# The second half of a transformer block dealt out again over five engines: gate rows, up weights, rotation, ada_t pages

## The reference

```python
mod = silu(c) @ ada_w + ada_b
shift1, scale1, gate1, shift2, scale2, gate2 = split(mod)
h = rms_norm(x, norm1_gain) * (1 + scale1) + shift1
r_q, r_k, r_v, r_g, s_q, s_k, s_v = split(h @ w_in)          # 7 x 512 columns
y_ret = head_group_norm(retention(rotary(r_q), rotary(r_k), r_v)) * silu(r_g)
y_sb  = rms_norm(stick_breaking(norm(s_q), norm(s_k), s_v))  # weights from log sigmoids
x = x + gate1 * (concat(y_ret, y_sb) @ w_out)
h2 = rms_norm(x, norm2_gain) * (1 + scale2) + shift2
x = x + gate2 * peer(h2, w_query, sub_keys, expert_down, expert_up)
```

## Time and profile before

| | |
|---|---|
| median of 3 runs | 1330.65 us (1329.43 to 1332.24) |
| profiled execution, its own time | 1334.88 us |
| its span, first to last instruction | 1333.1 us |
| busy share of PE, DVE, ACT, POOL | 96, 74, 55, 23% |
| mean granted clock of PE | 0.976 of full |
| PE's share of the chain that ended last | 91% |
| DMA share in 200 to 240, 240 to 260 us | 0.90, 0.96 |
| waits of PE from 200 to 600 us | none over 0.1 us |

### The profile page before, as it was taken

One profiled execution on the slowest core, in us unless ns is written; L12 is line 12 of the kernel. 1 busy time (PEld: TensorE's weight loads), 2 busy tenths in 40 slices (PEclk: granted clock), 3 DMA queues, 4 the chain that ended last, 5 costly groups with the idle time before them and its releaser, 6 DMA issues.

```text
span 1333.1 us, 19834 instructions
## 1 busy us (share of the span) xinstructions
PE 1273.6 (96%) x7918; PEld 1135.7 (85%) x7918; DVE 991.3 (74%) x1714; ACT 729.2 (55%) x1130; POOL 302.8 (23%) x186
## 2 busy tenths in 40 slices
PE   3797989999999999999999999999989999999998
PEld 3675879999999999999888888888877788899996
DVE  6988878889999889994767777676676465755554
ACT  3664544555555599993554444455455455554443
POOL 0135100088876887540000000000000022000000
PEclk8898999999999999999999999999989997999999
DMA  9964659877777778889887878787654441555551
GB/s 369 358 245 171 217 178 324 308 223 237 237 221 226 225 220 281 271 275 350 332 306 272 303 272 303 274 293 281 225 183 157 161 163 40 189 184 193 184 189 77
DMA packets 138286, 317.10 MB, mean 238 GB/s; under 512 B 24783, under 2 KB 71120, under 8 KB 132306
## 3 DMA queue, kind: packets, MB, share of 16 engines
q1 hardware_dynamic: 101106, 265.42, 55.4%
q0 software_dynamic: 23072, 16.86, 6.7%
q10 hardware_dynamic: 14016, 33.56, 6.6%
HBM read 280.61 MB, written 35.20 MB: 237 GB/s over the span
## 4 chain that ended last, share of the span: by engine, by line
PE 91%; DVE 5%; DMA 1%; ACT 1%; issue 1%; DVEq 0%; SPq 0%; ACTq 0%
PE ps L632 12%; PE ps L633 11%; PE ps L634 11%; PE ps L645 11%; PE ps L644 11%; PE ps L646 11%; PE ps L610 3%; PE ps L611 3%; PE ps L612 3%; PE ps L922 1%; PE ps L974 1%; DVE arena L1729 1%; DMA wring<-in_peer_up 1%; PE ps L993 1%; DVE pages L1729 1%; DVE w_lo L1649 1%
## 5 line engine op out<-in xcount | busy, mean ns | idle before, releaser
L1649 DVE TENSOR_TENSOR w_lo<-wring,w_hi 128x1024 fp32r<-128x1024 f32 (+1 forms) x404 | 492.6, 1225 | 173.6 <-ACT w_hi L1184 169.6
L1184 ACT CAST w_hi<-wring 128x1024 fp32r<-128x1024 f32 (+1 forms) x404 | 418.9, 1044 | 247.2 <-PE ps L634 148.2
L632 PE MATMUL ps<-hT_hi,w_hi 128*128 128x256 f32 x1344 | 377.8, 281 | 0.0
L634 PE MATMUL ps<-hT_hi,w_lo 128*128 128x256 f32 x1344 | 377.5, 281 | 0.0
L633 PE MATMUL ps<-hT_lo,w_hi 128*128 128x256 f32 x1344 | 377.4, 281 | 0.0
L1601 POOL DMA_INDIRECT gates_of_second<-late x128 | 245.8, 1920 | 134.8 <-DMA gates_of_second<-zeros 55.1
L634 PEld LDWEIGHTS ps<-hT_hi,w_lo 128*128 128x128 f32 x1344 | 256.0, 190 | 0.0
L644 PE MATMUL ps<-w_hi,a_hi 128*128 128x512 f32 x640 | 251.8, 393 | 2.7 <-DVE w_lo L1649 2.7
L632 PEld LDWEIGHTS ps<-hT_hi,w_hi 128*128 128x128 f32 x1344 | 253.9, 189 | 0.3
L645 PE MATMUL ps<-w_lo,a_hi 128*128 128x512 f32 x640 | 252.7, 395 | 0.0
L633 PEld LDWEIGHTS ps<-hT_lo,w_hi 128*128 128x128 f32 x1344 | 252.5, 188 | 0.2
(11 more groups left out here) (316 smaller groups left out, 1466.5 us busy)
## 6 DMA issues: line engine op xcount, KB each, us to landing
wring<-in_peer_down SPq DMA_DIRECT2D x32, 2048.0 KB
wring<-in_peer_up SPq DMA_DIRECT2D x32, 2048.0 KB
wring<-in_w_in SPq DMA_DIRECT2D x12, 2048.0 KB
pages<-in_ada_t POOLq DMA_DIRECT2D x32, 512.0 KB, 5.0
acts_by_expert<-pages ACTq DMA_DIRECT2D x32, 512.0 KB
peer_arena<-acts_by_expert SPq DMA_DIRECT2D x32, 512.0 KB, 8.7
wring<-in_w_up SPq DMA_DIRECT2D x8, 2048.0 KB
wring<-in_w_down SPq DMA_DIRECT2D x8, 2048.0 KB
```

The source lines that it names most:

```text
L632: pe.matmul(o, hi[:, k, :], hT_hi[:, k, :], start=(k == 0), stop=False)
L634: mm = pe.matmul(o, lo[:, k, :], hT_hi[:, k, :], start=False, stop=(k == KC - 1))
L1184: act.copy(split_part(kind, w_hi, u, width(kind, j)), part_of(kind, wring[:, n % RING, :], u, width(kind, j))).then_inc(split_hi, 1)
L1649: dve.tensor_tensor(lo, part_of(kind, wring[:, n % RING, :], u, width(kind, j)), hi, ALU.subtract)\
```

## The change

Ten or so pieces of work change places; the arithmetic stays.

- The pages come in another order: gate1 first, then shift2 and scale2 in two halves, then gate2. The second modulation is made in two halves (`late_modulation`), the second one between the halves of `h_round(3)`.
- POOL's second block of the rotation waits for the second group's `sb_logs`.
- PE makes three parts of R_V, not two, before `log_stays(1)`; R_G's first part goes ahead of the rotated turn, its second behind it; `turn_y(0)` goes ahead of `kept_values(1)`; the rows of gate1 go from between the output parts to behind `turn_y(1)`, those of gate2 from the query products to behind down product 18.
- ACT and DVE splits follow. DVE's `h_round(2, half 0)` goes ahead of the sums over the retention values.
- SP issues the first up weights before the wait for `gates_added` and before the second table's first piece.

The diff, cut to the places that the prediction speaks of:

```diff
-LATER_TILES = [*range(3 * KC, 5 * KC), *range(2 * KC, 3 * KC), *range(5 * KC, 6 * KC)]
+LATER_TILES = [*range(2 * KC, 3 * KC), *[which * KC + half * KC // 2 + k for half in range(2) for which in (3, 4) for k in range(KC // 2)],
+               *range(5 * KC, 6 * KC)]
...
                 acts_back(j)
-            sp.wait_ge(gates_added, 16 * PK * PH)
-            second_gates_back(0)
             for u in range(2):
                 sp.wait_ge(gates_stored[u], 16 * (P // 32))
             first_gates_back(0)
             weights(NTH["ex", 0])
+            sp.wait_ge(gates_added, 16 * PK * PH)
+            second_gates_back(0)
+            first_gates_back(1)
             second_gates_back(1)
-            first_gates_back(1)
             weights(NTH["ex", 1])
...
-            by_tokens("win", R_V, parts=[0, 1])
+            by_tokens("win", R_V, parts=[0, 1, 2])
             log_stays(1)
...
             stick_values(0)
-            token_parts("win", R_V, [2, 3])
+            token_parts("win", R_V, [3])
+            by_tokens("win", R_G, parts=[0])
             pe.wait_ge(S["rot_ready"], 2)
...
             turn_round(lambda k, b: h_tok[:, b, k * P:(k + 1) * P], KC)
-            by_tokens("win", R_G, parts=[0])
+            token_parts("win", R_G, [1])
             copied(2)
             head_scores(4, 0).then_inc(S["ret_scores"], 1)
             stick_values(1)
-            token_parts("win", R_G, [1])
             pe.wait_ge(S["ret_decayed"], 1)
             head_scores(4, 1).then_inc(S["ret_scores"], 1)
+            token_parts("win", R_G, [2])
             kept_values(0)
-            token_parts("win", R_G, [2, 3])
-            kept_values(1)
+            token_parts("win", R_G, [3])
+            pe.wait_ge(S["ret_decayed"], 2)
             pe.wait_ge(S["y_ready"], 1)
             turn_y(0)
+            kept_values(1)
             h_stands(2, 0)
-            out_part(0, 0)
-            out_part(0, 1)
-            gate_rows(M_GATE1, 4, 1)
-            out_part(0, 2)
+            for u in range(PARTS):
+                out_part(0, u)
             pe.wait_ge(S["y_ready"], 2)
             turn_y(1)
-            out_part(0, 3)
+            gate_rows(M_GATE1, 4, 1)
             h_stands(2, 1)
...
-                if j == 1:
-                    gate_rows(M_GATE2, 6, 2)
-                if j == 2:
-                    pe.wait_ge(S["gate_out"], 2)
                 key_scores(j - 1)
...
+            pe.wait_ge(S["sub_out"], 4)
+            gate_rows(M_GATE2, 6, 2)
             pe.wait_ge(S["sel_ready"], PH)
...
-            h_round(3, gain=column(modc, M_SCALE2), shift=column(modc, M_SHIFT2))
+            h_round(3, gain=column(modc, M_SCALE2), shift=column(modc, M_SHIFT2), only=0)
+            act.wait_ge(S["mod_ready"], 4)
+            h_round(3, gain=column(modc, M_SCALE2), shift=column(modc, M_SHIFT2), only=1)
...
+                if b == 1:
+                    pool.wait_ge(S["sb_ls"], 2)
                 own(pool.tensor_tensor(dst[:, :, 0, :], src[:, :, 0, :], cos, ALU.mult))
...
+            def late_modulation(half):
+
+                first, count = half * KC // 2, len(FIRST_TILES) + (half + 2) * KC
+                take_columns(M_SHIFT2 + first, M_SHIFT2 + first + KC // 2, count)
+                own(take_columns(M_SCALE2 + first, M_SCALE2 + first + KC // 2, count))
+                modulation(half + 3, M_SCALE2, G_2, first, KC // 2)
...
             dve.wait_ge(S["ret_y_out"], 2)
...
-            h_round(2, only=0)
             dve.tensor_tensor(yr, yr, over_heads(4), ALU.subtract).then_inc(S["y_centered"], 1)
...
             split("wout", 1, parts=[2, 3])
+            sum_pages(3)
+            late_modulation(0)
...
-                if b == 1:
+                if b == 0:
+                    sum_pages(1)
+                else:
                     dve.wait_ge(S["x1_ready"], 2)
...
             split("wq", 0, parts=[1])
+            sum_pages(1)
             h_round(3, gain=column(modc, M_SCALE2), shift=column(modc, M_SHIFT2), only=0)
             split("wq", 0, parts=[2, 3])
+            sum_pages(3)
+            late_modulation(1)
             h_round(3, gain=column(modc, M_SCALE2), shift=column(modc, M_SHIFT2), only=1)
```

More of the change, by code:

```diff
@@ L1290, in _ @@
             weight_exp(0)
-            split("win", R_V, parts=[1])
+            split("win", R_V, parts=[1, 2])
             log_break(1)
-            split("win", R_V, parts=[2, 3])
+            split("win", R_V, parts=[3])
             take_win(S_V)
@@ L1409, in _ @@
                     take_scores(3)
+                if j == TURN_AFTER:
+                    act.wait_ge(S["gate_turned"], 2)
+                    act.copy(GATE2, psf[:, 6 * 512:6 * 512 + D]).then_inc(S["gate_out"], 1)
                 if j >= 1:
@@ L1856, in _ @@
             sb_mask(0)
-            split("win", R_V, parts=[1])
-            sum_pages(2)
+            split("win", R_V, parts=[1, 2])
             sb_logs(1)
-            split("win", R_V, parts=[2, 3])
+            split("win", R_V, parts=[3])
             sum_pages(1)
@@ L1894, in _ @@
             dve.tensor_tensor(ys, ys, head_gain(2), ALU.mult).then_inc(S["y_ready"], 1)
+            split("wout", 0, parts=[0])
+            sum_pages(2)
+            h_round(2, only=0)
             split("wout", 0, parts=[1])
-            sum_pages(1)
             dve.wait_ge(S["ret_y_out"], 2)
```

42 lines of the change are left out of this document (17 added, 25 removed).

## The result

The changed kernel took 1314.9 us, median of four runs (1312.8 to 1318.8), beside 1330.0 for the one before: ratio 0.9888, 95% interval 0.986 to 0.9917. The forecast was 1324.0 in a range of 1318 to 1330. In two later samples of the same kernel the medians were 1323.6 (11 runs, ratio 0.9936, 0.9906 to 0.9966) and 1318.3 (12 runs, 0.9927, 0.9892 to 0.9963). Over all 28 runs the median is 1318.3, against 1329.7 over 93 later runs of the kernel before (one of 1551 left out). The gain is real in each sample. That it is larger than the forecast's 6.6 (a ratio of 0.995) is clear in the first sample alone; the intervals of the two later ones hold 0.995 as well. Most of this text is on where the rest comes from.

What follows compares the result with a forecast made beforehand. TensorE, busy 96% of the span, was taken as the bound, so only its waits and low-clock stretches counted. The terms summed to -6.6, from 1330.65 to 1324.0 us, range 1318 to 1330.

Steps and rivals of the forecast that it cites:

- Terms 1 to 4: Second logarithm's wait gone -8.8; first output product's wait gone -4.3; out_block's new wait +1.0; pages in DVE's slots +0.2.
- Term 5: First query product: PE waits 2.4 for hT_lo behind three pages and half a modulation, then low clock 1.7; +4.1.
- Term 6: Up weights: the second gates' first piece, now issued behind them, delays weighing and ACT's start before the up-projection; +1.2.
- at no cost: Pages, gate rows and GATE2's copy same in number; GATE2's rows move behind down product 18, where PE has no waits.
- the stall hidden (1): DVE runs ahead, so the wait for hT_lo in the first query weight is hidden; 1320.0 us, chance 0.16.
- the head start lost (2): Transfers rather than PE set the pace between 200 and 260, so time won earlier is waited away; 1329, chance 0.13.
- the lock (3): Shared-port lock lengthens the second rotation and margins at output product and out_block are missed; 1328.5, at worst 1332; chance 0.10.
- the late gates (4): First up product waits for gates_of_second's piece, landing more than 20.5 after issue; slower, 1334; chance 0.07.

Runs made afterwards that it cites:

- a_no_pool_wait: The changed kernel without POOL's wait for sb_ls ahead of its second rotation; 1322.9 us in one run.
- b_gate2_late: The kernel before with only GATE2's row products and ACT's copy moved behind down product 18; 1323.4 us (10 runs), ratio 0.9964.
- b_rows_behind: The kernel before with GATE2's row products behind the first key scores instead of ahead of them; 1317.5 us in one run.
- b_gate2_late2: b_gate2_late profiled and timed again; 1328.3 us (12 runs), ratio 0.998.
- a_pages_rows_early: a_pages_out with GATE2's row products, ACT's copy and PE's wait for it back between the query products; 1318.5 us (8 runs), ratio 0.9923.
- a_rows_extra: The changed kernel with a second, unused set of GATE2's 8 row products at their old place between the query products; 1329.1 us (10 runs), ratio 1.0012.
- a_pages_out: The changed kernel with SP's old order at the up weights and two page sums moved from between h_round(3)'s halves to earlier slots; 1312.7 us (four runs).
- a_again: The changed kernel, unaltered, profiled a second time and timed again; median 1323.6 us.

## Why the prediction was wrong

Its walk was right and its total was not. None of the three signs that it named as its own refutation came: out_block started at 165.7 and not later than 168, a stall stood within the first query weight, and from 210 to 600 PE had no wait. By its own steps:

- **Terms 1 to 4**, -8.8 - 4.3 + 1.0 + 0.2 = -11.9. Measured in a to c: before 105.8 to 106.1, after 93.7, so -12.1 to -12.4. The logarithm's last products (L1812) ended at 114.2 instead of 112.7, of which 1.5 is that this execution came to its first logarithm later (94.25 against 92.79 in before); the rotation ended at 125.65 and PE turned it at 126.14. Out_block began at 165.73 against 164.7, and waited 0.57. From the exclusive lock on the shared port in the Trainium skill ("SBUF - State Buffer", section "SBUF: two separate sides") the prediction had concluded that the place of the rotation would be no matter and the sum 3.9 worse. Both sides are in fact lengthened where they overlap (a page sum takes 2.3 and not 1.2, most steps of the rotation 2.1 and not 1.3), but the conclusion isn't borne out: the rotation took 11.4 and not 14.4, and its place is worth the 2.8 of a_no_pool_wait.
- **Term 5**, +4.1. Measured in c to d: 25.3 less the 1.8 of the rows is 23.5, as b_gate2_late and b_rows_behind show; after 27.5 to 28.1: +4.0 to +4.6. The size was right. The make-up, 2.4 of waiting for hT_lo with a low clock behind it, was right in half of the ten profiles of this walk (2.0 to 2.2). In the other half, the first profile among them, it was another: 1.0 of waiting and no fall of the clock behind it, but half clock for 5.9 in the first half of the weight, and 1.3 at the second weight, where three of four page sums ahead of the split of its weight waited for their transfers (0.95 together).
- **Term 6**, +1.2. Measured in e to f, where d-e's step has no part: 150.6 to 151.7 before, 152.1 to 153.5 in four profiles of after: +1.7. The piece landed 13.2 after its issue; second_gates_back(0) ahead again gives 150.5 to 151.6 in five profiles. (The 630.80 of the prediction, for the landing of the weights, stands in no row; ACT's wait for them ended at 630.86. That transfers start in order doesn't settle in which order they land either.)
- **The sum of these** is -12.2 + 4.3 + 1.7 = -6.2 against the forecast's -6.6. The timed runs agree: a_gate2_early, the change with GATE2's rows left where they were, is 6.8 under before (interval of the ratio 0.9915 to 0.9973, or 3.6 to 11.3 us).
- **The step that failed is "at no cost"**: that GATE2's rows move to a place where PE has no waits, so that the move has no term in the sum. Timed, the move alone is worth 4.6 (b_gate2_late and b_gate2_late2 together, 22 runs, median 1325.1), and 6.8 and 4.6 make up the 11.4 between the medians over all runs. Waits weren't what the rows cost. Before comes to them with the short step, turns to the long one and keeps it to the end of the stage: 258.5 (its 3 transposes turn it back for the last 14 us). Moved away, the short step stays: 251.4, which holds the 1.8 of the rows as well. In three of four profiles of after that is -7.1 more; in the fourth, which entered long, 260.8, +2.3. If the upper and lower group of the 28 runs are these two (11 and 17), the mean is (17 x -7.1 + 11 x 2.3) / 28 = -3.4, and with the walk's -6.2 it is -9.6. Medians over all runs give -11.4, means 1320.9 - 1329.7 = -8.8.
- **A second fault is in the method**: the forecast went by the spans of one execution. The stages that the change doesn't touch (g-h 174.9 to 182.6, to end 153.5 to 156.0) differ together by up to 9 between executions. In the two kernels' first profiles these alone made -9 of the difference of 22. And that the first median was as low as 1314.9 was in part luck: all four of its runs lie in the changed kernel's lower group, which has 17 of 28.
- **Rivals**: of the stall hidden (1), the head start lost (2), the lock (3) and the late gates (4), none took place. The result's low side was no rival's.

That the early rows are the cause of before's long step is shown for profiles, 7 turns of 7. That they cost time is shown less firmly: of the intervals of b_gate2_late and b_gate2_late2 one excludes no change and the other doesn't. That the step is how they cost it is argued only, and two things on record speak against it as the whole account. a_pages_rows_early, where the rows turned the step to short, isn't faster for it. And up to the rows b_gate2_late is the program of before: eleven of the 22 runs of it lie under 1324, and if the other eleven came to the rows with the long step, the rows should turn it to short in half of before's runs too, but seven of 93 lie under 1324. Open stays why an execution leaves the first query weights with one step or the other, why rows ahead of key scores turn it and rows behind them don't, and why the transposes turned it back in before (3 of 3) and not in a_gate2_early.

## What to carry to other kernels

When a stage of hundreds of equal products is bound by PE, count products per microsecond in it before and after at the same granted clock, in more than one profile: 4% of step over 250 us is 9 us, more than any wait of PE in this text. A short run of unlike products put into such a stream isn't priced by its own duration. And where the single times of a kernel fall into two groups, four runs can't tell 1315 from 1324; time both kernels some ten times or more before a gain under 1% is believed.

## What the runs showed of the hardware that was not expected

- 256-column products have two steps at granted clock 1.00: 179 or 172 in 20 us, 0.113 or 0.118 from start to start. Within a stage the step was constant over hundreds of products; it changed where other products stood between them, or across a wait (0.4 in the four profiles with pages moved out). From the first spread product on it was the long one in all 20 profiles. The same program showed both.
- 512-column products had a second step too, 0.2333 in place of 0.2289: all through the up-projection of a_rows_extra (f-g 362.8), and in the first expert weight of the second block in eight profiles.
- The second block's expert products vary in the same way, and this is the whole difference in the table's last column: 156.0 with the long step throughout, 153.5 with the short one, 153.7 where it turned from long to short behind the first 512-column weight. 10 us within one 256-column weight in before and in a_pages_out:

```profile
1205.00:1215.00 10.00, 10.00 (x87) 10.00 (x86) 6.58 (x8) 6.11 (x9) 0.00 (x0) 1.00 0.58 207
```
```profile
1195.40:1205.40 10.00, 10.00 (x90) 10.00 (x90) 6.84 (x8) 6.15 (x9) 0.00 (x0) 1.00 0.57 207
```

- Waits of 0.8 and 1.5 in a_no_pool_wait, and of 1.0 and 1.3 in after, were followed by full clock. Those of 2.0 to 2.2 for hT_lo in five profiles were followed by a low one (0.53 over 3.6 us in a_again). The half clock in after came behind 3.2 of waiting for diag and 3.1 more.
